# Compress folded into the projection's last tile, attention's first heads loaded into w_in's end, and no clearing of the score tile

## What is computed

```python
parts = jnp.split(h @ w_in[l], split_points, axis=-1)          # h = rms_norm(x); 1720 columns
y_mla = mla_mixer(cq, ckv, krope, ...)                          # 8 heads, dense causal attention
y_nsa = nsa_mixer(q_nsa, kc, vc, ks, vs, kw, vw, ...)           # compressed, selected and window branches

def compress_blocks(t, cmp_idx, pos_emb, w1, w2):               # kc and vc, 2 groups of 64 columns each
    blk = t[:, cmp_idx] + pos_emb[None, None, :, None, :]       # 63 blocks of 32 tokens, 16 apart
    hid = jax.nn.gelu(jnp.einsum('bnlgd,ldf->bngf', blk, w1))   # w1: 32 x 64 x 128
    return jnp.einsum('bngf,fd->bngd', hid, w2)                 # w2: 128 x 64
...
k_cmp = rms_norm(compress_blocks(kc, ...), g_k)
v_cmp = compress_blocks(vc, ...)
```

## Time and profile before

| | us |
|---|---|
| median of 3 runs | 3165.4 |
| lowest, highest | 3160.09, 3167.91 |
| the profiled execution | 3161.41 |
| its span, first to last instruction | 3159.4 |
| mean granted TensorE clock | 0.942 |

### The profile page before, as it was taken

One profiled execution on the slowest core, in us unless ns is written; L12 is line 12 of the kernel. 1 busy time (PEld: TensorE's weight loads), 2 busy tenths in 40 slices (PEclk: granted clock), 3 DMA queues, 4 the chain that ended last, 5 costly groups with the idle time before them and its releaser, 6 DMA issues.

```text
span 3159.4 us, 41652 instructions
## 1 busy us (share of the span) xinstructions
PE 2775.9 (88%) x12040; PEld 1389.2 (44%) x12041; DVE 1121.8 (36%) x2925; ACT 593.6 (19%) x1582; POOL 220.6 (7%) x188
## 2 busy tenths in 40 slices
PE   6998599999789963899999899999998999899895
PEld 3555456666455541343444343433333344344332
DVE  2766267767536642223222121221222222122221
ACT  1222155555423310001001010010001000000000
POOL 0000000000001101100000101010110010100110
PEclk9999599999899965999999999999999999999998
DMA  8322563030212116857556777587877676745870
GB/s 294 78 61 69 116 174 90 1 90 15 80 35 68 41 40 225 332 184 281 181 174 219 298 287 249 177 288 263 305 288 260 240 247 236 286 172 176 299 285 14
DMA packets 294757, 570.21 MB, mean 180 GB/s; under 512 B 78878, under 2 KB 117790, under 8 KB 274184
## 3 DMA queue, kind: packets, MB, share of 16 engines
q1 hardware_dynamic: 255805, 530.28, 47.2%
q0 software_dynamic: 21152, 38.52, 5.4%
q10 hardware_dynamic: 17707, 0.22, 0.3%
HBM read 542.67 MB, written 69.88 MB: 194 GB/s over the span
## 4 chain that ended last, share of the span: by engine, by line
PE 50%; issue 4%; DMA 3%; DVE 2%; ACT 1%; ACTq 1%; POOL 0%; POOLq 0%; DVEq 0%
PE ps L1815 28%; PE ps L1899 17%; PE ps L1911 3%; DMA out<-ys_e,dst 2%; PE ps L1788 2%; DVE gu L1716 1%; PE ps L1793 1%; ACT aT L1634 1%; DMA xg<-d_h,src 1%; ACT xT_e L1614 0%; DVE gg L1719 0%; ACTq L1527 0%; DMA src<-d_tok 0%; POOL out L1596 0%; DVE ys_e L1758 0%
## 5 line engine op out<-in xcount | busy, mean ns | idle before, releaser
L1815 PE MATMUL ps<-wg,xT_e 128*64 128x512 f32 (+2 forms) x4032 | 1035.8, 599 | 33.4 <-issue 30.0
L1815 PEld LDWEIGHTS ps<-wg,xT_e 128*64 128x64 f32 (+2 forms) x4032 | 400.7, 147 | 638.1 <-issue 634.0
L1899 PE MATMUL ps<-w_rows,aT 128*128 128x512 f32 x1152 | 529.2, 614 | 41.7 <-issue 24.6
L1716 DVE TENSOR_TENSOR gu<-ps,bias 64x512 f32<-64x512 f32 (+2 forms) x252 | 173.7, 689 | 595.6 <-PE ps L1815 563.9
L1899 PEld LDWEIGHTS ps<-w_rows,aT 128*128 128x128 f32 x1152 | 220.3, 196 | 311.5 <-issue 287.6
L1656 ACT ACTIVATE ss<-gg 128x256 f32<-128x256 f32 x146 | 60.9, 417 | 1293.6 <-issue 708.0
L1760 DVE TENSOR_SCALAR ys_e<-ps,dst 128x1024 f32<-128x1024 f32 x36 | 46.2, 1284 | 623.4 <-PE ps L1899 623.4
L1596 POOL DMA_INDIRECT out<-ys_e,dst x64 | 102.0, 1593 | 1452.1 <-DVE ys_e L1760 952.6
L442 PE MATMUL ps<-w_in,hT_a 128*128 128x430 f32 x512 | 193.4, 530 | 6.3 <-DVE hT_a L345 6.3
L793 PE MATMUL ps<-ident_t,sc 128*128 128x128 f32 x880 | 151.3, 289 | 29.7 <-ACT sc L859 26.2
L859 ACT ACTIVATE sc<-sc,nm 128x640 f32<-128x640 f32 (+15 forms) x256 | 161.9, 635 | 53.9 <-DVE nm L901 53.9
(11 more groups left out here) (293 smaller groups left out, 2453.3 us busy)
## 6 DMA issues: line engine op xcount, KB each, us to landing
wg<-in_w_gate_up SPq DMA_DIRECT2D x128, 2048.0 KB, 8.4
w_rows<-in_w_down SPq DMA_DIRECT2D x128, 1024.0 KB
bias<-in_b_gate_up SPq DMA_DIRECT2D x32, 1024.0 KB, 9.4
d_bias<-d_rev SPq DMA_DIRECT2D x1, 10368.0 KB, 37.9
w_in<-in_w_in SPq DMA_DIRECT2D x1, 6880.0 KB, 25.0
x_a<-in_x POOLq DMA_DIRECT2D x8, 512.0 KB, 3.9
kn<-d_kn SPq DMA_DIRECT2D x8, 512.0 KB
strip_t<-d_bias SPq DMA_DIRECT2D x8, 512.0 KB
```

The costliest lines, as they stand in the source:

```text
L1716: read = dve.tensor_tensor(gu[part, :], ps[part, BANK[k][j], :], bias[part, cols], ALU.add)
L1815: mm = pe.matmul(ps[g * kind:(g + 1) * kind, BANK[k][j], :], xT[:, kk, t0:t0 + kind], wg[:, j * groups + g, kk, :], start=(kk == 0), stop= ...
L1899: mm = pe.matmul(ps[:, 2 + 2 * b + h, :], aT[:, j, b * P:(b + 1) * P], wd[:, c, j % 2, h * 512:(h + 1) * 512], start=(j == 0), stop=(j == ...
```

## The change

Three things are done. (1) The block compress is gone. Its matmuls stand in the project block, between the steps of tile 7: the turning of that tile's compress columns and of the position rows (`turn_last`, while tile 6's bank 0 is free) ahead of `turn_c`; 80 of the 128 products between `turn_n` and `turn_q`; the other 48, the two `second` steps and the turning of the keys behind `turn_q`. The last 160 columns of cnT come by an ACT copy from PSUM in place of the DMA. The bias `pb` is copied by ACT. The position rows are loaded at the block's start. (2) w_in is held in two tiles, five of its eight slices in `w_in` and the last three in `w_in_end`, loaded by two DMAs. `ident_t`, `mstrip` and `cvalid` are loaded in tile 1; queries, keys and values of the first two heads go into the memory of `w_in_end` by four DMAs at the very end of the project block (`load_first_heads`). (3) POOL's clearing of `sc` and DVE's wait for it are gone.

```diff
+    for dst, src in ((e.ident_a[:, :], e.c_ident), (e.w_in_t[:, :, :], w_in[:, 0:KD - 3, :]), (e.w_in_end[:, :, :], w_in[:, KD - 3:, :]),
...
+                    if t == 1:
+                        load_first(nc, e, sp)
...
-                    sp.dma_start(e.cnT[:, :, rows], nT[b][:, 6:8, :]).then_inc(s_st[b], 16)
+                    if t < NT - 1:
+                        sp.dma_start(e.cnT[:, :, rows], nT[b][:, 6:8, :]).then_inc(s_st[b], 16)
...
+                sp.wait_ge(s_kT, 1)
+                sp.dma_start(e.d_ck.rearrange("g d n -> d g n"), kT[:, :, :]).then_inc(s_out, 16)
+                sp.wait_ge(s_cc, 1)
+                sp.dma_start(e.d_cv.rearrange("g n d -> n g d"), cc[:, G:, :]).then_inc(s_out, 16)
                 for b in range(2):
-                    sp.wait_ge(s_st[b], 160 * (NT // 2))
+                    sp.wait_ge(s_st[b], 160 * (NT // 2) - 16 * b)
+                load_first_heads(e, sp)
+                sp.wait_ge(s_out, 32)
...
+                        hidden(0)
...
+                def hidden(i):
+                    act.wait_ge(s_cmp, i + 1)
+                    act.activation(pb[:, i:i + 1], ps[:, CMP_BANK[i][0], NCMP + 1:NCMP + 2], ACT.Copy).then_inc(s_pb, 1)
+                    act.wait_ge(s_pb, i + 1)
+                    for g in range(G):
+                        act.activation(hid[:, i, g * NCMP:(g + 1) * NCMP], ps[:, CMP_BANK[i][g], 0:NCMP], ACT.Gelu_apprx_tanh, bias=pb[:, i:i + 1]).then_inc(s_hid, 1)
...
+                    if t == NT - 1:
+                        act.wait_ge(s_last, 1)
+                        act.activation(e.cnT[:, :, t * P:], ps[:, 0, 0:2 * (P + CMP_LEN)].rearrange("p (i n) -> p i n", i=2), ACT.Copy).then_inc(s_cnT, 1)
...
+                act.wait_ge(s_ssqc, 1)
+                act.activation(stc[:, :], stc[:, :], ACT.Sqrt, bias=eps[0:NCMP, 0:1], scale=1.0 / HD).then_inc(s_stdc, 1)
+                hidden(1)
...
+                dve.wait_ge(s_w2, 1)
+                ch(dve.tensor_copy(cc[:, 0:G, :], ps[0:NCMP, 1, 0:G * HD].rearrange("p (g d) -> p g d", d=HD)))
...
+                dve.wait_ge(s_kTp, 1)
+                dve.tensor_copy(kT[:, :, :], ps[0:HD, 2, 0:G * P].rearrange("p (g n) -> p g n", g=G)[:, :, 0:NCMP]).then_inc(s_kT, 1)
+                dve.wait_ge(s_w2, 2)
+                dve.tensor_copy(cc[:, G:, :], ps[0:NCMP, 3, 0:G * HD].rearrange("p (g d) -> p g d", d=HD)).then_inc(s_cc, 1)
...
+                def turn_last():
+                    t, b = NT - 1, (NT - 1) % 2
+                    pe.wait_ge(s_pos, 16 * 2 * G)
+                    pe.wait_ge(s_prD, t + 1)
+                    pe.wait_ge(s_qA, t)
+                    pe.wait_ge(s_qD, t)
+                    for i in range(2):
+                        at = i * (P + CMP_LEN)
+                        pe.transpose(ps[:, 0, at:at + P], pr[b][:, C_KC + i * P:C_KC + (i + 1) * P], ident[:, :])
+                        mm = pe.transpose(ps[:, 0, at + P:at + P + CMP_LEN], pos[:, i, :, :].rearrange("p g d -> p (g d)"), ident[0:CMP_LEN, 0:CMP_LEN])
+                    mm.then_inc(s_last, 1)
+
+                def products(i, ls):
+                    if ls[0] == 0:
+                        pe.wait_ge(e.cmp_in[i], 16 * N_CMP)
+                        pe.wait_ge(s_cnT, 1)
+                        pe.wait_ge(s_st[0], 160 * (NT // 2))
+                        pe.wait_ge(s_st[1], 160 * (NT // 2 - 1))
+                    for l in ls:
+                        for g in range(G):
+                            half = slice(g * HD, (g + 1) * HD)
+                            mm = pe.matmul(ps[:, CMP_BANK[i][g], 0:NCMP + 2], w1[half, i, l, :], e.cnT[half, i, l:l + S + 1:CMP_STRIDE],
+                                           start=(l == 0), stop=(l == CMP_LEN - 1))
+                    if ls[-1] == CMP_LEN - 1:
+                        mm.then_inc(s_cmp, 1)
+
+                def second(i):
+                    pe.wait_ge(s_hid, G * i + G)
+                    for g in range(G):
...
+                    if not more:
+                        turn_last()
                     turn_c(t)
...
+                    else:
+                        products(0, range(CMP_LEN))
+                        products(1, range(CMP_LEN // 4))
                     turn_q(t)
...
+                second(0)
+                products(1, range(CMP_LEN // 4, CMP_LEN))
+                pe.wait_ge(s_ck, 1)
+                for g in range(G):
+                    mm = pe.transpose(ps[0:HD, 2, g * P:g * P + NCMP], cc[:, g, :], ident[0:NCMP, 0:NCMP])
+                mm.then_inc(s_kTp, 1)
+                second(1)
...
+def load_first_heads(e, sp):
+    sp.dma_start(e.qm_first, e.d_qm[0:2].rearrange("h d n -> d h n")).then_inc(e.first_in, 16)
+    sp.dma_start(e.km_first, e.d_km[0:2].rearrange("h d n -> d h n")).then_inc(e.first_in, 16)
     for h in range(2):
-        sp.dma_start(e.vm_t[:, 0, h, :, :], e.d_vm[h].rearrange("(t p) d -> p t d", p=P)).then_inc(e.first_in, 16)
...
-                pool.memset(sc[:, :, :, :], 0.0).then_inc(s_set, 1)
...
-                dve.wait_ge(s_set, 1)
-                dve.wait_ge(e.first_in, 16 * N_FIRST_MLA)
+                dve.wait_ge(e.strip_in, 48)
```

184 lines of the change are left out of this document (62 added, 122 removed).

## The result

| | before | after |
|---|---|---|
| median of 5 runs each | 3161.13 | 3137.34 |
| lowest, highest | 3159.75, 3167.91 | 3124.84, 3144.76 |
| the profiled execution, its span | 3161.41, 3159.4 | 3124.84, 3123.1 |
| mean granted TensorE clock of it | 0.942 | 0.950 |

The changed kernel is faster: ratio 0.9914, 95% interval 0.9888 to 0.9941. It was measured twice more, each time beside runs of the kernel before: 0.9902 (0.9888 to 0.9917) and 0.9919 (0.9899 to 0.9939). All its 15 runs have a median of 3136.1, the 53 runs of the kernel before one of 3163.2: 27.1 us (23.8, 28.8 and 28.5 in the three comparisons). The forecast was 3135, or 28.3 us off; 3163.2 less 28.3 is 3134.9.

The account below looks back on a forecast made before the run. From 312 to 410 us a chain of waits, mostly not TensorE, was taken as the bound. The later shift, gates' 28.7 us less 0.4 of setup, gave 28.3 us and a forecast of 3135, range 3126 to 3147.

Parts of the forecast that it names:

- Setup, 0.4: Project block's start: one more DMA to issue on SP, taken as 0.4 us later; the early loads cost 0.
- Cover ahead of turn_c: Tile 7 ahead of turn_c: four small turnings and an ACT copy cost 0, or about 1.5 us without cover.
- 80 products in the wait: Between turn_n and turn_q: 64 products take 6.9 us, 16 take 1.7, cost 0 with 0.6 us of slack.
- turn_q at 3.5: Turning of tile 7's queries: kept at the old 3.5 us, with 1.5 us as a possible gain.
- The last chain: Behind turn_q: second 0.7, 48 products 5.2, then copy, 1.28 table load, Gelu, w2; d_cv issued by 353.3 us.
- The heads' loads, 12.2: End of project block: first heads' loads land 12.2 us after first issue, at 365.5; block ends at 358.7.
- First peak group: Start of attention: scores from 365.6, unit 0's last peak ends at 372.6 us, 29.6 earlier.
- gates, the step that was off: Landing of gates behind thirteen transfers: 381.0 us, 28.7 earlier, between bounds of 375.9 and 382.7.
- High clock throughout: Rival: turn_q takes 1.95 us and the first scores 3.5, gain about 33, 3130 us; chance 0.15.
- Low clock: Rival: the products fall to or start at 1.2 GHz, later terms move 12.2 us, gain 16, 3147; chance 0.15.
- Slower: Rival: attention stays at 1.2 GHz after PE's 16 us idle; 60 us of it would give 3185; chance 0.03.
- The change doesn't do what it says: Case that products are not hidden in tile 7's gaps, tied to the low clock's 3147 us; chance 0.15.

Follow-up runs that it names:

- no_clearing: The kernel before with only the clearing of sc and DVE's wait for it removed: 3161.6 us, ratio 0.9992.
- warm_and_early: The changed kernel with gates issued first, first scores awaiting only queries and keys, idle TensorE matmuls before them, and an early Gelu table load: 3126.7 us, ratio 0.9886.
- warm_products: products_behind with ten idle 128x512 matmuls added in TensorE's wait ahead of turn_q, results unused: 3140.3 us, ratio 0.9932.
- after_again: The changed kernel, unaltered, measured a second time beside the kernel before: 3135.4 us, ratio 0.9902.
- after_third: The changed kernel, unaltered, measured a third time beside the kernel before: 3134.7 us, ratio 0.9919.
- products_behind: The changed kernel with all 128 products behind turn_q and none in the gap ahead of it: 3151.3 us, ratio 0.9951.

## Why the forecast held, step by step

1. *Setup, 0.4.* Not to be told. Project starts at 47.98 in the profile after and at 47.28 in that of before, but at 46.68 and 46.95 in the two later ones of the changed kernel and at 46.77 in no_clearing. The spread is larger than the term.

2. *Cover ahead of turn_c.* Held: the first matmul of `up` starts at 321.46 (320.92 in the earlier trace rows), 0.5 later with a project that began 0.7 later.

3. *80 products in the wait.* Right in kind, with two terms off. 64 took 7.50 us, not 6.9, and the 16 took 2.18, not 1.7: the high clock makes these records 1.84 times as fast (27.57 against 256 x 0.0586 = 15.0), about the factor that the 16 turnings gave, not the 2 that was taken. The longer 64 cost nothing, since TensorE then waited for the values' weights. These landed 10.5 us behind their issue, at 338.7, where the step took the 9.6 of the earlier trace rows and 337.8, though the position rows had left that queue (one line's instructions, L626, and its landing):

```profile
L626 SPq DMA_DIRECT2D w_in<-in_cmp_v_w x1: 4682/4682/4682, 328.2 to 328.2; - x1
...
DMA to landing us min/median/max: 9.9/10.2/10.5
```

The 0.9 of the landing and the 0.5 of the 16 use up the 0.6 us of slack, and `turn_q` begins 0.3 us behind DVE's last result (340.55). In warm_and_early, with the 16 at the low clock, it is 2.5.

4. *turn_q at 3.5.* 3.39, most of it at the low clock, as was assumed. Behind the dense matmuls of warm_products it took 1.95.

5. *The last chain.* From the start of `turn_q` to `d_cv` 12.27 us against 13.2: the products 5.69 against 5.2, `second` 0.44 against 0.7 (it ran at the high clock too), the chain behind them 2.9 against 3.8 with hand-overs. The table's load of 1.28 was on the path; the activation began 0.02 behind it (351.74 against 350.44 + 1.28), and taking it away gave back 1.28. The Trainium skill, "ScalarE: Activation LUTs", section "What ACT_TABLE_LOAD costs", would have 2.66 with a drain; this trace shows no such drain here, neither in the row nor in the gain.

6. *The heads' loads, 12.2.* 11.3 from first issue to last landing (353.47 to 364.73), in after_again 11.0. The block's end at 358.04 was forecast at 358.7.

7. *First peak group.* 372.44 against 372.6. Two small errors offset each other: the loads landed 0.8 sooner than forecast (364.73), and from the first score to the end of the last peak it took 7.6 us, not 7.0.

8. *gates, the step that was off.* 381.0 was forecast, 378.21 came. The step took the thirteen NSA loads as beginning nearly only when the heads' loads were through. The row shows what they cost them instead: SP's first issue sits 3.88 us, and `gates` is used 20.2 us after the block's start in place of 17.2. So two groups in one queue overlap, and the later one paid 3.0, not 5.1 (22.3 from 358.7 to 381.0, less 17.2). It fell inside the bounds of 375.9 and 382.7.

The sum of the steps in the trace is 31.5 us at the use of `gates`, not 28.3; the medians show 27.1. The profiled runs of the changed kernel that came later have 378.26 and 377.65 there, so the 31.5 is no accident of one run. Behind that place the profiled execution took 4.8 us less than that of before to the end of its span, after_again's and after_third's 7.4 and 1.1 more (2757.1 and 2750.7, against 2749.7). At DVE's last record of attention the three profiles of the changed kernel are 31.3, 28.1 and 29.3 us sooner than that of before (813.14, 816.39 and 815.19 against 844.48). The units of attention themselves, use of `gates` to that record, took 434.7 before and 437.1 in no_clearing, and 434.9, 438.7 and 436.9 in the three profiles of the changed kernel. By stretch, from 400 us (430 in the kernels before) to attention's end, the clock reads 1.00 in the profile after and 0.99 in the two later ones, 1.00 in those of before. Falls of the clock are thus of the size of the difference in question, and five traces don't say whether some 4 us are given back there or not. It stays open. That the forecast of 3135 comes so close is in part luck: step 8 put the gain at its mark 3 us too low, and the medians show some 4 us less than the traces do there, which no step of the sum had.

The rivals. *High clock throughout* was half right: the products had it, `turn_q` and the scores not. *Low clock* is what products_behind shows when it does come to that, and it gives 3151 there, since all 128 run low and none is hidden. *Slower*, attention stuck at 1.2 GHz, didn't occur: at 371 the clock was up, 6 us behind the first score. *The change doesn't do what it says* holds for one of its three parts: leaving the clearing out was worth nothing, which the sum had, since it counted to `gates`.

The prediction weighed a rule of the Trainium skill ("TensorE: Matmul & The Clock Gate", section "Why this matters for your kernels", that a TensorE kept continuously busy comes to its full clock) against the row at 0.50. products_behind shows the row again, 27.00 of 27.00 us busy at 0.50. For matmuls of 64 rows and 65 columns the rule doesn't hold in these traces, and what the assumption of the sum needed, that they hold a high clock, is now measured.

## What to carry to other kernels

Ask of a wait not how long it is but what comes last once it is gone: 10.20 us of waiting for the clearing were worth nothing, because a small load in the thirteenth place of a queue landed after it. Ask the same of that load: moving it to the front took 1.54 us from the next mark and 0.2 from the one behind. Read a gain at the first place that everyone waits for, not at the wait that was taken away. Work that TensorE does at a low clock may gain more from what stands ahead of it than from being hidden; look at the granted clock of the stretch before pricing its move. In a DMA queue, put the small thing that others wait for ahead of the large, split the large by what is ready early, and wait for each reader's own part.
